# Keeping the residual token-major in a ten-stage fp32 transformer block: wide second products, transposes between stages, norm sums from accumulators

## What is computed

```python
def rms_norm(x, g):
    y = x * lax.rsqrt(jnp.mean(x * x, axis=-1, keepdims=True) + EPS)
    return y * g

x = x + mixer(rms_norm(x, g_mix))                      # pa, rg, hy0, hy1
x = x + (gelu(conv(h @ w_gate)) * (h @ w_up)) @ w_down # ffn0, ffn1, hf0, hf1; h = rms_norm(x, g_ffn)

# inside the hybrid mixer:
merged = gates[:, :, 0] * (o_mla @ w_branch[0]) + gates[:, :, 1] * (o_diff @ w_branch[1]) \
       + gates[:, :, 2] * (o_win @ w_branch[2])        # gates = sigmoid(h @ w_gates)
x = x + merged @ w_out

e = rms_norm(pe @ w_ple_proj, g_ple)                   # ple0, ple1
x = x + sigmoid(rms_norm(x, g_ple_in) @ w_ple_gate) * e
```

## Time and profile before

| | |
|---|---|
| median of 3 runs | 1837.67 us (1836.41 to 1839.14) |
| span of the profiled execution | 1832.0 us |
| PE busy | 1719.5 us, 94% |
| PE weight loads busy | 1622.7 us, 89% |
| DVE, ACT, POOL busy | 1115.7, 917.4, 163.4 us |
| DMA | 259.27 MB, mean 142 GB/s |
| weight units | 239, split by ACT in 1910 ns and DVE in 2311 ns each |

### The profile page before, as it was taken

The page is one execution under the profiler, slowest core; times in us unless marked ns, Lnnn a source line. Parts: engine busy times, 40 slices in busy tenths (PEclk is TensorE's granted clock), DMA queues, the critical chain, the costliest instruction groups (busy, mean ns, idle before and its releaser), DMA issues.

```text
span 1832.0 us, 31411 instructions
## 1 busy us (share of the span) xinstructions
PE 1719.5 (94%) x13040; PEld 1622.7 (89%) x13040; DVE 1115.7 (61%) x1332; ACT 917.4 (50%) x1225; POOL 163.4 (9%) x98
## 2 busy tenths in 40 slices
PE   6989999787899999999999999998999999999998
PEld 6789999787899989778889999998968878999997
DVE  4537777677677776557336666565556634666665
ACT  4346454677454545525453644455434635444444
POOL 0030111000011110000012100000000002110000
PEclk9899999899899999979999999998978999999999
DMA  6324555434255544412224455543421223455551
GB/s 249 103 85 150 194 184 175 163 133 157 79 191 191 184 137 142 142 44 97 84 92 167 161 184 179 189 138 116 161 92 63 94 75 116 146 184 185 179 187 67
DMA packets 36251, 259.27 MB, mean 142 GB/s; under 512 B 4144, under 2 KB 4272, under 8 KB 5040
## 3 DMA queue, kind: packets, MB, share of 16 engines
q1 hardware_dynamic: 35712, 255.86, 40.8%
q10 hardware_dynamic: 432, 1.84, 0.3%
HBM read 256.63 MB, written 1.05 MB: 141 GB/s over the span
## 4 chain that ended last, share of the span: by engine, by line
issue 47%; PE 40%; DVE 5%; ACT 4%; POOL 2%; DMA 1%; POOLq 0%; SPq 0%; ACTq 0%; DVEq 0%
PE bank L1340 9%; PE bank L1341 8%; PE bank L1342 8%; PE bank L1506 4%; PE bank L1543 2%; PE bank L1491 2%; DVE w_lo L795 2%; PE bank L1524 2%; ACT w_hi L386 1%; PE bank L1384 1%; POOL h_lo L1273 1%; POOL y_lo L1273 1%; DMA raw<-W 1%; PE bank L1475 1%; PE bank L1388 1%
## 5 line engine op out<-in xcount | busy, mean ns | idle before, releaser
L1340 PE MATMUL bank<-h_hi,w_hi 128*128 128x256 f32 x2640 | 764.7, 290 | 34.7 <-DVE w_lo L795 15.3
L795 DVE TENSOR_TENSOR w_lo<-raw,w_hi 128x2048 fp32r<-128x2048 f32 x239 | 552.4, 2311 | 353.0 <-ACT w_hi L386 352.3
L1341 PE MATMUL bank<-h_lo,w_hi 128*128 128x256 f32 x2640 | 754.5, 286 | 0.0
L1342 PE MATMUL bank<-h_hi,w_lo 128*128 128x256 f32 x2640 | 754.0, 286 | 0.0
L386 ACT ACTIVATE w_hi<-raw 128x2048 fp32r<-128x2048 f32 x239 | 456.5, 1910 | 357.8 <-PE bank L1342 327.0
L1340 PEld LDWEIGHTS bank<-h_hi,w_hi 128*128 128x128 f32 x2640 | 514.0, 195 | 56.7 <-issue 33.5
L1341 PEld LDWEIGHTS bank<-h_lo,w_hi 128*128 128x128 f32 x2640 | 514.4, 195 | 0.3
L1342 PEld LDWEIGHTS bank<-h_hi,w_lo 128*128 128x128 f32 x2640 | 513.9, 195 | 0.0
L1340 PE MATMUL bank<-y_hi,w_hi 128*128 128x256 f32 x1040 | 298.4, 287 | 28.2 <-POOL y_lo L1273 27.3
L1342 PE MATMUL bank<-y_hi,w_lo 128*128 128x256 f32 x1040 | 296.0, 285 | 0.0
L1341 PE MATMUL bank<-y_lo,w_hi 128*128 128x256 f32 x1040 | 294.2, 283 | 0.0
(11 more groups left out here) (200 smaller groups left out, 1466.1 us busy)
## 6 DMA issues: line engine op xcount, KB each, us to landing
raw<-W SPq DMA_DIRECT2D x239, 1024.0 KB, 4.9
wide<-RW ACTq DMA_DIRECT2D x1, 1280.0 KB, 5.5
con<-CON SPq DMA_DIRECT2D x1, 1258.0 KB, 9.8
x<-XT SPq DMA_DIRECT2D x1, 1024.0 KB, 5.2
OUT<-x SPq DMA_DIRECT2D x1, 1024.0 KB, 3.9
wide<-CON SPq DMA_DIRECT2D x1, 768.0 KB, 14.5
val<-PE_T ACTq DMA_DIRECT2D x2, 256.0 KB, 4.8
vec<-VEC SPq DMA_DIRECT2D x1, 394.0 KB, 3.2
```

The costliest lines, as they stand in the source:

```text
L795: V.tensor_tensor(w_lo[:, n0 % NW], raw[:, n0 % NRAW], w_hi[:, n0 % NW].bitcast(F32), ALU.subtract)\
L1340: T.matmul(out, w[0], a[0], start=start, stop=False, **kw)
L1341: T.matmul(out, w[0], a[1], start=False, stop=False, **kw)
L1342: return T.matmul(out, w[1], a[0], start=False, stop=stop, **kw)
```

## The change

- x becomes token-major, `[128, 2, 1024]`: two tiles of 128 tokens with all features. `xs(b)` is the piece of token tile b%2 and feature half b//2 that bank b holds.
- `onto` turns round: 128 tokens of the activations are stationary, 512 weight columns stream; 24 matmuls a unit. The banks are finished in the same order, a quarter of the unit each.
- At each stage head the PE transposes x back in 16 pieces of 128x128 (`turned`): pairs 0 and 1 between the third and the fourth bank of the last `onto` unit, pairs 2 and 3 inside the first unit of the next stage. ACT and DVE make `h_hi`, `h_lo` from PSUM.
- ACT squares x with an accumulator, which gives sums for each token; DVE adds two columns, ACT takes the root, DVE the reciprocal, all on `[128, 2]` (`rc`). `normed` now broadcasts `rc` into a row with two products and waits for it.
- The hybrid stages' gate units go token-major too. Their gates are half of 1 + tanh(z/2), taken by ACT straight from PSUM in the attention; DVE's scalings of them and the six sigmoids are gone. The merged sum is transposed by the PE (`merged`); its low parts are made by DVE instead of POOL.
- In `ple` the embedding's norm sums come from accumulators, its gain is broadcast by the PE, and the gates' scaling moves into ACT's sigmoid.
- At the start the PE transposes the input (16 pieces), at the end the output (16 pieces), which leaves in four transfers.

```diff
@@ tensor: onto
-                for m in range(8):
-                    if begin and m % 2 == 0 and free:
-                        acc_free(pe, s, j, m // 2)
+                for b in range(4):
+                    if begin and free:
+                        acc_free(pe, s, j, b)
+                    tok = slice((b % 2) * P, (b % 2) * P + P)
                     for k in range(2):
-                        last = three(bank[m // 2][:, (m % 2) * S:(m % 2 + 1) * S], cols(n, k * 1024 + m * 128, 128),
-                                     act_parts[k], begin and m % 2 == 0 and k == 0, end and k == 1, skip_group_check=True)
+                        hi, lo = act_parts[k]
+                        last = three(bank[b][:], (hi[:, tok], lo[:, tok]), cols(n, k * 1024 + (b // 2) * 512, 512),
+                                     begin and k == 0, end and k == 1)
...
+                    if b in (between or {}):
+                        between[b]()
@@ tensor: first_unit
                 for k in range(8):
+                    if k == 2 and NORM[s]:
+                        turned(s, (2, 3))
@@ tensor: new, and normed
+            def turned(s, js):
+                k = NORM[s]
+                for j in js:
+                    pe.wait_ge(sems["x_up"], 4 * k + 2 * (j // 2) + 2)
+                    if j >= 2:
+                        pe.wait_ge(sems["h_ready"], 4 * k + j - 1)
+                    for t in (2 * j, 2 * j + 1):
+                        for kt in range(2):
+                            o = (t % 2) * S + kt * P
+                            m = T.transpose(bank[6 + j % 2][:, o:o + P], x[:, kt, t * P:(t + 1) * P], c_("ident"))
+                    m.then_inc(sems["tp_done"], 1)
             def normed(s):
                 k = NORM[s]
...
-                for t in range(8):
-                    pe.wait_ge(sems["sq_ready"], 4 * k + t // 2 + 1)
-                    m = T.matmul(bank[6][:, 0:S], ones, sq[:, t], start=t == 0, stop=t == 7)
...
+                pe.wait_ge(sems["rc_done"], k + 1)
+                for kt in range(2):
+                    m = T.matmul(bank[6][:, kt * P:(kt + 1) * P], rc[:, kt:kt + 1].broadcast_to([P, P]), c_("ident"),
+                                 start=True, stop=True)
                 m.then_inc(sems["st_done"], 1)
@@ scalar: norm
+                    square(0)
+                    square(1)
+                    high(0)
+                    high(1)
+                    square(2)
+                    square(3)
+                    high(2)
+                    high(3)
...
+                act.wait_ge(sems["ss_done"], k + 1)
+                nc.scalar.activation(rc[:], rc[:], ACT.Sqrt, bias=eps, scale=1.0 / D).then_inc(sems["rms_done"], 1)
                 after(B[s] - 1)
...
+                    nc.scalar.activation(rinv, bank[6][:, 0:S], ACT.Copy).then_inc(sems["rinv_done"], 1)
@@ vector: onward, norm
-                behind = {0: [], 1: [0], 2: [1], 3: [2, 3]}
+                behind = {0: [], 1: [], 2: [0], 3: [1, 2, 3]}
...
+                dve.wait_ge(sems["sq_done"], 4 * k + 4)
+                V.tensor_tensor(rc[:], ss[:, :, 0], ss[:, :, 1], ALU.add).then_inc(sems["ss_done"], 1)
                 after(B[s] - 1)
                 dve.wait_ge(sems["rms_done"], k + 1)
-                V.reciprocal(rinv_t[:, 0:w], rinv_t[:, 0:w]).then_inc(sems["rinv_done"], 1)
+                V.reciprocal(rc[:], rc[:]).then_inc(sems["rc_done"], 1)
@@ vector: hy, behind the branch sums
                     after(ub + 26 + 2 * b)
+                for j in range(4):
+                    dve.wait_ge(sems["h2hi"], 4 * atts.index(s) + j + 1)
+                    V.scalar_tensor_tensor(out=pair(h_lo, j), in0=bank[4 + j][:], scalar=0.5, in1=pair(h_hi, j).bitcast(F32),
+                                           op0=ALU.mult, op1=ALU.subtract).then_inc(sems["h2_ready"], 1)
@@ tensor: hy
-                        onto(s, b, ub + 25 + p, y_parts(p % 2), j == 0, j == 1)
+                        onto(s, b, ub + 25 + p, y_parts(p % 2), j == 0, j == 1,
+                             between={2: lambda: merged((0, 1))} if p == 5 else None)
+                merged((2, 3))
```

More of the change, by code:

```diff
@@ L211, in build, with row_no @@
         ples = [s for s in used if kind(s) == "ple"]
+        def row_no(s):
+            return sum(kind(a) != "ple" for a in used[:used.index(s) + 1])
         def scaled_before(s):
@@ L399, in norm, with high @@
                 k = NORM[s]
-                for j in range(4):
+                def high(j):
                     if k == 0:
@@ L1028, in pa @@
                 norm(s)
+                row(s)
                 for e in range(5):
@@ L1732, in ple @@
                 pe.wait_ge(sems["pe_ready"], L + 1)
-                onto(s, 0, ub, y_parts(1), True, True)
-                normed(s)
-                pe.wait_ge(sems["ple_ev"], 8 * L + 4)
-                for t in range(8):
-                    m = T.matmul(bank[7][:, 0:S], ones, wide[:, 8 + t], start=t == 0, stop=t == 7)
-                m.then_inc(sems["est_done"], 1)
+                onto(s, 0, ub, y_parts(1), True, True, between={0: lambda: turned(s, (2, 3))})
+                for dh in range(2):
+                    pe.wait_ge(sems["h_ready"], 4 * NORM[s] + 3 + dh)
+                    for t in range(4):
+                        m = T.matmul(bank[6 + dh][:, t * P:(t + 1) * P],
+                                     v_(f"g_ple{s[-1]}", 4 * dh + t).broadcast_to([P, P]), c_("ident"), start=True, stop=True)
+                    m.then_inc(sems["grow_done"], 1)
                 for j in range(4):
```

231 lines of the change are left out of this document (152 added, 79 removed).

## The result

The changed kernel takes **1860.68 us** (median of 4 runs, 1857.92 to 1865.98) against 1837.26 (1836.41 to 1839.14) of the kernel before on the same chip: ratio 1.0126, 95% interval 1.0107 to 1.0145, so 23 us or 1.3% slower. 1860.5 had been forecast. The profiled execution spans 1858.5 us against 1832.0.

The account below looks back on a forecast made before the run. PE was taken as the bound, busy 94% of the span. Terms -6 + 10.7 + 4.2 - 6 + 19 - 6.4 - 4.3 + 11.6 = +22.8 us on 1837.7 gave 1860.5; 8-in-10 range 1838 to 1882.

Parts of the forecast that it names:

- the signs named: Trace marks to expect: 512-column starts 0.234 us apart, PE idles at heads and merges, late `hy1` second unit, more half clock.
- the prediction's walk: Engine timelines followed through `ffn0`'s head: second unit at 152.9, 2.8 us late; other places by the same walk.
- Second products, -6: `onto` units with 24 matmuls of 512 columns at 0.234 us: 0.04 less on 63 units, 0.18 on 20; -6 us.
- The rival at 0.2155 us: Wide products stream at 0.2155 us like fp32 rows, stalls stay: sum -14, 1823.5 us, faster; chance 12%.
- Five heads, +10.7: Heads of `ffn0`, `rg`, `ffn1`, `hf0`, `hf1`: +1.6, +2.4, +1.9, +2.4, +2.4 us from the wait for `rc`; +10.7 us.
- `hy0`, +4.2: Head of `hy0`: DVE's position geometry delays the sum of squares, against 3.6 us more of statistics that go; +4.2 us.
- `hy1`, -6: Head of `hy1`: shorter end of `ple0` and the new chain put its second unit 6 us earlier; -6 us.
- The merges, +19: Two merges: first `w_out` product waits for DVE's low part behind a weight split, about 9.5 us late each; +19 us.
- `ple`, -6.4: Two `ple` stages: statistics rows go, transposes and gain broadcast come, -3.2 us each; -6.4 us with rounding.
- Start, -2.8: Kernel start: second unit waits for `rc` at 26.8 us instead of for statistics until 30; -2.8 us.
- End, -1.5: Kernel end: output leaves in four 256 KB transfers as pieces come instead of one of 1 MB; -1.5 us.
- Clock, +11.6: New idles at heads, merges, start, `hy0` and `hy1` can each cost 1.7 us in slow clock; +11.6 us, ends 0 and 20.

Follow-up runs that it names:

- 1: Changed kernel with DVE taking the reciprocal of `rc` ahead of its weight split at each stage head; 1832.96 us, ratio 0.9974 against the kernel before.
- 2: Changed kernel with DVE making the four `h_lo` ahead of the split of unit `ub+33` at both merges; 1843.34 us, ratio 1.0032 against the kernel before.
- experiment 5: Changed kernel with the input's transfer ahead of the identity's at the start; 1864.97 us, ratio 1.0143 against the kernel before.
- experiment 4: Kernel before with one addition: PE waits for the reciprocal behind each stage head's statistics; 1879.52 us, ratio 1.0233.
- 12: Changed kernel with both DVE reorderings, reciprocal ahead of the split at heads and `h_lo` ahead of it at merges; 1824.5 us, ratio 0.9936 against the kernel before.
- experiment 7: Changed kernel with the splits of `ub+32` and `ub+33` both behind `h_lo` at the merges; 1842.58 us, ratio 1.0025 against the kernel before.

## Why the prediction was right, and its terms

The forecast of 1860.5 met 1860.7, and the signs named came: idle of 2.5 us ahead of the broadcast released by DVE's reciprocal, 2.85, 1.51 and 5.46 at the merges with the split ahead of the last, more half clock. The two mechanisms were tested by taking each away (1 and 2). But several terms were mis-sized, and they cancel. The terms below are measured from starts, over the same places that the prediction's walk used; "without the clock" takes off the half-clock time in them.

- *Second products, -6.* Measured -9.6 to -10: y units 0.05 shorter as taken, h units 0.32 in place of 0.18. The rival at 0.2155 us had 12% and fell: the starts are 0.227 to 0.236 apart. The row of the same form and type was the better guide than the fp32 row. The rule quoted from the Trainium skill ("TensorE: Matmul & The Clock Gate", section "Back-to-back issue gap"), 216 ns at 512 columns, stays below every unit measured here, by 5% for h units and 8% for y units, so here the measured pace counts.
- *Five heads, +10.7.* Too high. From the start of the last unit of the stage before to the fourth unit, and without the clock, the traces give 1.3 at `ffn0`, 1.8 at `rg`, 1.1 at `ffn1`, 0.9 at `hf0` and 1.5 at `hf1`: +6.5. At `ffn0` the walk was right: from the last unit's start the root is there after 13.7 us (13.9 by hand) and the second unit starts after 18.4 (18.9), 2.2 late and not 2.8. That all of it stands 1.4 us earlier on the clock than in the walk comes from `pa`, which ends 1.2 earlier. The later heads were set too high: their second units are 1.9 to 2.2 late, and at three of the four the fourth unit takes back another 0.7 to 1.0.
- *`hy0`, +4.2:* +3.7 to the third unit, without the clock. Right, with an idle of 7.8 us in it.
- *`hy1`, -6:* -2.2, from the start of `ple0`'s last unit to the second unit of `hy1` (27.61 before, 25.46 now), or -2.9 without the clock. The second unit starts 20 us behind the end of `ple0`, not 16: 4.51 us of idle stand ahead of the transposes and 1.57 ahead of the first unit, which then runs at half clock.
- *The merges, +19:* 10.8 each, of which 1.3 and 1.5 are half clock, so +18.8 without the clock: the best-founded term. The three idles had been put at 3, 1.6 and 6.
- *`ple`, -6.4:* -3.3 and -3.5, so -6.8 without the clock, from the last feed-forward unit's start to the second unit. The parts that the prediction lists come to -3.0 each and not to the -3.2 that it takes.
- *Start, -2.8:* -0.2 at the second unit, since the input's transfer came 2.5 us later behind the identity's, which the walk had left out (experiment 5); -0.8 without the clock. *End, -1.5:* -0.9 from the last unit's start.
- *Clock, +11.6:* +16.6 by the starts, with the 2.3 us that the record before leaves out, and inside the range of 0 to 20 given for it. With the heads it is the largest miss. In experiment 4, 18 us of half clock came with 30 us of gaps.

Without the clock these terms sum to +8. The savings of the wide product in single units that lie inside the measured places stand in the sum twice, 2 us; without that it is +10, which is what the spans give (26.5 less 16.6). The forecast had 11.2 there, by a gain of the wide products that was 3.6 too small and heads that were 4.2 too dear on one side, and on the other by a `hy1` that was 3.1 and a start that was 2.0 too cheap. With the clock it had 22.8, against 26.5 between the spans and 23.4 between the medians. The spans differ by more since the profiled execution of the kernel before lies 5.3 us under its median of 1837.26 and that of the changed kernel 2.2 under its own; the forecast took the same 5.7 for both. That the total fell within 0.2 us is luck, of signs and of this offset. That it was slower by 1 to 2% is not: the heads and merges were read from the order of two streams, and experiments 1 and 12 turn the result round by changing that order.

What stays open: why an h unit gains 0.32 us by width and a y unit 0.05 at the same shape, and what sets the half-clock stretches in and ahead of the attentions, which move the total by several microseconds between kernels.

## What to carry to other kernels

When an engine that never waited is made to wait for a value, walk the producer's stream back from that value: a 0.16 us instruction behind a 4.2 us piece of background work, at each stage head, cost 28 us, by the traces 15 in waits and 12 in the slow clock, more than the 23 by which the change is slower. Put the background piece into a time in which its engine waits anyway, and check at the next stage that it isn't late there (experiment 7). Price a wait of the PE with the slow clock behind it, and judge a restructuring only after its new waits have been ordered: the same change is 1.3% slower as it came and 1.4% faster with some twenty lines moved.

## What was not expected of the hardware

- Matmuls of 512 columns in fp32r start 0.234 us apart in y units and 0.227 in h units; those of 256 columns 0.118 and 0.120. The order of the two kinds turns round with the width.
- An fp32 product of 128 columns by 128 is two rows, 0.224 us together; a transpose of the same size is one row, 0.11.
- A unit of 5.44 us took 8.23 behind an idle of 5.46, and 5.58 when 44 rows of useless products filled that idle.
